# The first extra pass of an expert standing by itself, and a pass's four banks signalled one by one

## The reference

```python
    for e in range(N_EXPERTS):
        h = jax.nn.silu(t @ w1[e]) * (t @ w3[e])
        out = out + gates[:, e:e + 1].astype(t.dtype) * (h @ w2[e])
```

## Time and profile before

| | us |
|---|---|
| runs shown, median of 3 | 1896.12 |
| lowest, highest | 1895.49, 1898.88 |
| the profiled execution, its own time | 1899.83 |
| its span, from first to last instruction | 1897.9 |
| PE busy | 1732.2 (91%) |
| PEld busy | 896.1 (47%) |
| DVE busy | 684.4 (36%) |
| ACT busy | 455.2 (24%) |
| POOL busy | 148.5 (8%) |

### The profile page before, as it was taken

The page is one execution under the profiler, slowest core; times in us unless marked ns, Lnnn a source line. Parts: engine busy times, 40 slices in busy tenths (PEclk is TensorE's granted clock), DMA queues, the critical chain, the costliest instruction groups (busy, mean ns, idle before and its releaser), DMA issues. The chain is left out here.

```text
span 1897.9 us, 24245 instructions
## 1 busy us (share of the span) xinstructions
PE 1732.2 (91%) x9138; PEld 896.1 (47%) x9138; DVE 684.4 (36%) x1403; ACT 455.2 (24%) x894; POOL 148.5 (8%) x113
## 2 busy tenths in 40 slices
PE   8998979998898888889899998999989998899996
PEld 7866643333574443333344544333358767433332
DVE  3344462221415562222312226222144435542223
ACT  2674211111214111111211101111123934111111
POOL 1024100000300100000020100000030131100000
PEclk9999989999999889999999998999999999899998
DMA  9521069999932369679964327899983220589994
GB/s 336 186 108 46 27 268 403 426 425 425 339 144 108 126 269 382 251 313 424 405 236 162 126 115 329 327 424 425 423 304 140 109 90 2 200 351 427 425 426 191
DMA packets 86426, 505.08 MB, mean 266 GB/s; under 512 B 8515, under 2 KB 16756, under 8 KB 59388
## 3 DMA queue, kind: packets, MB, share of 16 engines
q1 hardware_dynamic: 75248, 488.65, 64.0%
q10 hardware_dynamic: 11020, 14.07, 2.2%
HBM read 501.64 MB, written 1.06 MB: 265 GB/s over the span
## 5 line engine op out<-in xcount | busy, mean ns | idle before, releaser
L2028 PE MATMUL bank<-ring,work 128*64 128x512 f32 x1280 | 371.5, 603 | 21.6 <-issue 21.6
L1543 DVE TENSOR_TENSOR work<-bank,work 64x512 f32<-64x512 f32 x64 | 67.9, 1061 | 525.0 <-ACT work L986 524.9
L1693 PE MATMUL bank<-HT,ring 128*128 128x256 f32 x1024 | 232.6, 387 | 0.0
L2028 PEld LDWEIGHTS bank<-ring,work 128*64 128x64 f32 x1280 | 119.5, 139 | 226.0 <-issue 225.5
L1693 PEld LDWEIGHTS bank<-HT,ring 128*128 128x128 f32 x1024 | 199.2, 195 | 37.4 <-issue 10.2
L2072 PE MATMUL bank<-ring,work 128*64 128x512 f32 x896 | 198.9, 595 | 0.0
L1701 PE MATMUL bank<-ring,HT 128*128 128x512 f32 x448 | 198.3, 602 | 0.0
L2028 PE MATMUL bank<-work 128*64 128x512 f32 x320 | 145.1, 603 | 0.0
L986 ACT ACTIVATE work<-bank 64x512 f32<-64x512 f32 x64 | 37.6, 588 | 437.3 <-PE bank L2028 437.3
L2028 PE MATMUL bank<-early_slot,work 128*64 128x512 f32 x320 | 140.7, 592 | 1.1 <-issue 1.1
L1701 PEld LDWEIGHTS bank<-ring,HT 128*128 128x128 f32 x448 | 85.7, 194 | 104.1 <-issue 104.1
(11 more groups left out here) (311 smaller groups left out, 1822.7 us busy)
## 6 DMA issues: line engine op xcount, KB each, us to landing
ring<-in_e_w SPq DMA_DIRECT2D x136, 2048.0 KB, 15.6
early_slot<-in_e_w SPq DMA_DIRECT2D x20, 2048.0 KB, 17.3
work<-in_e_w SPq DMA_DIRECT2D x20, 2048.0 KB, 18.4
ring<-in_a_w_in SPq DMA_DIRECT2D x15, 2048.0 KB, 19.7
work<-in_e_w SPq DMA_DIRECT2D x16, 1024.0 KB, 12.4
HT<-in_e_w SPq DMA_DIRECT2D x16, 1024.0 KB, 15.0
ring<-in_c_w_in SPq DMA_DIRECT2D x8, 2048.0 KB, 21.5
ring<-in_b_w_in SPq DMA_DIRECT2D x6, 2048.0 KB, 25.6
```

The source lines that it names most:

```text
L1543: v.tensor_tensor(by_m(h_[j]), bank[b][CAP:, :], sil[j][CAP:, :], ALU.mult).then_inc(drained[b], 1)
L1693: ins = mm(dst[:, 0:SEQ], wt[:, k, n * P:(n + 1) * P], HT[:, k, :], start=k == 0, stop=k == KC - 1)
L2028: ins = mm(bank[b][lo:lo + CAP, :], x[:, k, :], wt[k], start=k == 0, stop=k == KC - 1, skip_group_check=True)
```

## The change

The pass's code becomes a function, `one_pass(n)`, on each of the three engines. It is called once with n = 1 straight inside `if counted[j] > CAP`; behind that stands `if counted[j] > CAP + Q`, and in it the loop, from n = 2, with the old comparison and a second copy of the pass. A new semaphore, `pass_added`, counts the adds of banks: PE signals `baton` with each of its four last products (so a pass has 12 steps), DVE waits for one, adds that bank, signals `pass_added`, and so on to bank 7. PE and DVE keep a register `added` beside `steps_done`. `scatter` waits at bank b for the add of bank b only; `compact` and the end of `pair` on DVE wait for all. Four small memsets at the start on DVE give `pass_added` its first four counts.

```diff
-PASS_STEPS = 10
+PASS_STEPS = 12
...
+        pass_added = sem("pass_added")
...
# ACT
                         with act.If(counted[j] > CAP):
-                            with act.Fori(1, PASSES) as n:
-                                with act.If(counted[j] > n * Q + Q):
-                                    b0 = act.snap(steps_done)
...
+                            def one_pass(n):
+                                b0 = act.snap(steps_done)
...
+                            one_pass(1)
+                            with act.If(counted[j] > CAP + Q):
+                                with act.Fori(2, PASSES) as n:
+                                    with act.If(counted[j] > n * Q + Q):
+                                        one_pass(n)
# DVE, over_sel
-                        b0 = dve.snap(steps_done)
+                        b0, a0 = dve.snap(steps_done), dve.snap(added)
                         dve.wait_ge(baton, b0)
+                        dve.wait_ge(pass_added, a0)
# DVE, the pass
                         with dve.If(counted[j] > CAP):
-                            with dve.Fori(1, PASSES) as n:
-                                with dve.If(counted[j] > n * Q + Q):
-                                    with dve.If(n > 1):
-                                        over_sel(it, j, n)
...
-                                    dve.wait_ge(h_ready, 2 * nres)
-                                    dve.wait_ge(baton, b0 + (more + 9))
-                                    for b in range(4, 8):
-                                        ins = v.tensor_tensor(part(b), bank[b][:, :], part(b), ALU.add)
-                                    ins.then_inc(baton, 1)
-                                    dve.reg_add(steps_done, steps_done, PASS_STEPS + more)
+                            def one_pass(n):
+                                b0 = dve.snap(steps_done)
...
+                                dve.wait_ge(h_ready, 2 * nres)
+                                for b in range(4, 8):
+                                    dve.wait_ge(baton, b0 + (more + 5 + b))
+                                    v.tensor_tensor(part(b), bank[b][:, :], part(b), ALU.add).then_inc(pass_added, 1)
+                                dve.reg_add(steps_done, steps_done, PASS_STEPS + more)
+                                dve.reg_add(added, added, 4)
+
+                            one_pass(1)
+                            with dve.If(counted[j] > CAP + Q):
+                                with dve.Fori(2, PASSES) as n:
+                                    with dve.If(counted[j] > n * Q + Q):
+                                        over_sel(it, j, n)
+                                        one_pass(n)
...
-                    steps = dve.snap(steps_done)
-                    dve.wait_ge(baton, steps)
+                    a0 = dve.snap(added)
+                    dve.wait_ge(pass_added, a0)
# DVE, at the start
+            for tt in range(TT):
+                for n in range(2):
+                    v.memset(place[:, tt, E + n:E + n + 1], -1.0).then_inc(pass_added, 1)
+            dve.wait_ge(pass_added, 4)
# PE, scatter and compact
-                    steps = pe.snap(steps_done)
-                    pe.wait_ge(baton, steps)
+                    a0 = pe.snap(added)
                     pe.wait_ge(sel_ready, s + (ready + 3))
...
                             pe.wait_ge(drained[b], s + first[b])
+                            pe.wait_ge(pass_added, a0 + (b - 4))
...
-                    steps = pe.snap(steps_done)
-                    pe.wait_ge(baton, steps)
+                    a0 = pe.snap(added)
+                    pe.wait_ge(pass_added, a0 + 3)
# PE, the pass
                         with pe.If(counted[j] > CAP):
-                            with pe.Fori(1, PASSES) as n:
-                                with pe.If(counted[j] > n * Q + Q):
...
-                                            ins = mm(bank[4 + 2 * tt + nh][:, :], m_turned[rr, tt * P:(tt + 1) * P], m_y[rr, :], start=True, stop=True)
-                                    ins.then_inc(baton, 1)
-                                    pe.reg_add(steps_done, steps_done, PASS_STEPS + more)
+                            def one_pass(n):
...
+                                        mm(bank[4 + 2 * tt + nh][:, :], m_turned[rr, tt * P:(tt + 1) * P], m_y[rr, :], start=True, stop=True).then_inc(baton, 1)
+                                pe.reg_add(steps_done, steps_done, PASS_STEPS + more)
+                                pe.reg_add(added, added, 4)
+
+                            one_pass(1)
+                            with pe.If(counted[j] > CAP + Q):
+                                with pe.Fori(2, PASSES) as n:
+                                    with pe.If(counted[j] > n * Q + Q):
+                                        one_pass(n)
```

More of the change, by code:

```diff
@@ new lines, in one_pass @@
+                            def one_pass(n):
+                                b0 = dve.snap(steps_done)
+                                if lead:
+                                    dve.wait_ge(baton, b0 + 2)
+                                    v.tensor_tensor(m_x, bank[4][:, 0:SEQ].rearrange("p (k c) -> p k c", k=KC), columns(g_col, Q), ALU.mult).then_inc(baton, 1)
+                                    dve.wait_ge(baton, b0 + 3)
+                                    v.tensor_tensor(m_x, m_x, columns(b_col, Q), ALU.add).then_inc(baton, 1)
+                                dve.wait_ge(baton, b0 + (more + 3))
+                                v.tensor_tensor(by_m(m_h[:, 0:SEQ]), bank[5][CAP:, 0:SEQ], m_sil[CAP:, 0:SEQ], ALU.mult).then_inc(baton, 1)
+                                dve.wait_ge(h_ready, 2 * nres)
[4 more added lines that the diff above has]
+                                dve.reg_add(added, added, 4)
@@ L1602, in _ @@
             own.then(v.memset(starts[:, :], 0))
+            added = dve.alloc_register("added_dve")
+            dve.reg_mov(added, 4)
             v.memset(place[:, :, :], -1.0).then_inc(baton, 1)
             dve.wait_ge(baton, 1)
+            for tt in range(TT):
+                for n in range(2):
+                    v.memset(place[:, tt, E + n:E + n + 1], -1.0).then_inc(pass_added, 1)
+            dve.wait_ge(pass_added, 4)
             ht_chunks(0)
@@ L2152, in pair @@
                         with pe.If(counted[j] > CAP):
-                            with pe.Fori(1, PASSES) as n:
-                                with pe.If(counted[j] > n * Q + Q):
-                                    b0 = pe.snap(steps_done)
-                                    for b in range(4, 8):
-                                        pass_free(b)
-                                    pe.wait_ge(baton, b0 + 1)
-                                    if lead:
-                                        for k in range(KC):
-                                            for tt in range(TT):
-                                                ins = mm(bank[4][:, k * Q:(k + 1) * Q], XH[:, tt, k * P:(k + 1) * P], m_sel[:, tt, :], start=tt == 0, stop=tt == TT - 1)
-                                        ins.then_inc(baton, 1)
-                                        pe.wait_ge(baton, b0 + 4)
-                                    narrow_up(5, m_x, w1, w3).then_inc(baton, 1)
-                                    pe.wait_ge(baton, b0 + (more + 4))
-                                    narrow_turn(6).then_inc(baton, 1)
-                                    pe.wait_ge(baton, b0 + (more + 6))
-                                    w2 = weights(4 + j)
-                                    narrow_down(7, w2).then_inc(baton, 1)
-                                    pe.wait_ge(baton, b0 + (more + 8))
-                                    for tt in range(TT):
-                                        for nh in range(2):
-                                            rr = slice(nh * CAP, (nh + 1) * CAP)
-                                            ins = mm(bank[4 + 2 * tt + nh][:, :], m_turned[rr, tt * P:(tt + 1) * P], m_y[rr, :], start=True, stop=True)
-                                    ins.then_inc(baton, 1)
-                                    pe.reg_add(steps_done, steps_done, PASS_STEPS + more)
@@ new lines, in one_pass @@
+                            def one_pass(n):
+                                b0 = pe.snap(steps_done)
+                                for b in range(4, 8):
+                                    pass_free(b)
+                                pe.wait_ge(baton, b0 + 1)
+                                if lead:
+                                    for k in range(KC):
+                                        for tt in range(TT):
+                                            ins = mm(bank[4][:, k * Q:(k + 1) * Q], XH[:, tt, k * P:(k + 1) * P], m_sel[:, tt, :], start=tt == 0, stop=tt == TT - 1)
+                                    ins.then_inc(baton, 1)
+                                    pe.wait_ge(baton, b0 + 4)
```

(15 more changed lines are left out.)

22 lines of the change are left out of this document (7 added, 15 removed).

## The result

The changed kernel takes **1986.65 us** (median of 4, 1984.89 to 1994.27), the kernel before 1895.80 beside it; the ratio is 1.0483, 95% interval 1.0458 to 1.0508. The forecast was 1991.0, in a range of 1925 to 2070. The profiled execution took 1994.27 us, with a span of 1992.4 and a mean granted clock of 0.947; before it was 1897.9 and 0.961.

The account below looks back on a forecast made before the run. PE's matmuls were taken as the bound, the weight stream close behind. From the profiled 1899.8 us, -9.4 + 85 + 41 - 17.7 - 3.5 gave 1995, or 1991 us against the median; range 1925 to 2070.

Parts of the forecast that it names:

- The loop, -9.4 us: PE's idle behind the four extra passes, put down to five empty loop rounds each; all 9.4 us expected to go.
- The signals, register waits, second bodies of ACT and DVE at nothing: Extra waits on PE and second pass copies on ACT and DVE, costed at nothing, as hidden under queued matmuls or waiting.
- Jumps beyond two fetched blocks, +85 us: PE's jumps over the doubled pass: 49 would leave the fetched blocks, each losing 1.9 us in the mean; 85 us.
- The second jump of a pair, +41 us: PE's second jump comes while a fetch is under way; waiting for it would add 83 us, otherwise 0; middle taken, 41.
- Late weights swallowed, -17.7 us: PE's waits before up products in the last pairs of layers 0, 2 and 3, 17.7 us, vanish as PE runs later.
- Idle of kind (3), -3.5 us: PE's two idle times before the turn at L2036, 1.93 and 1.55 us, taken off as already in the jump count.
- The clock, nothing in the sum: Lower granted clock after PE idles of over 2.4 us: 1.5 us lost each for 25, counted only in rival (c).
- rival (c): Every second jump pays 3.3 us and long idles bring the clock down: about 2070 us, chance 0.12.
- Rival (a): PE's fetcher goes further ahead than two blocks, so longer jumps cost nothing more: 1889 us, faster, chance 0.10.
- Rival (b): Jumps miss but fetches take only 3.4 us, as weight traffic thins: about 1900 to 1915 us, chance 0.10.

Follow-up runs that it names:

- one_body_one_signal: Kernel before, with PE's loop made to end at the expert's count and one signal for all four banks kept: 1892.64 us, ratio 0.9989.
- first_only: Kernel after, with the second part (loop over passes 2 and on) left out on PE, ACT and DVE: 1882.02 us, ratio 0.9911.
- pe_one_body: Kernel after, but PE has one pass body in a loop ending at the expert's count; ACT and DVE keep two: 1888.26 us, again 1884.12.
- dead_half: Kernel before, with only one up-projection of a pass (140 instructions) as never-run copy on PE: 1951.39 us, ratio 1.0303.
- dead_copy: Kernel before, with a second, never-run copy of the pass body behind the loop on PE alone: 2018.71 us, ratio 1.0638.
- two_hops: Kernel after, with the second part on PE behind the first if instead of inside it, so two jumps over one body each: 2042.01 us, ratio 1.0725.

## Why the prediction was right, and where by luck

The sign, the mechanism and the total were right: 1986.65 against 1991.0. By its own steps:

- **The loop, -9.4 us**: -9.9 by start-to-start time. Right, and for the reason given: with the loop's rounds gone alone DVE's adds are late next, 2.22 and 2.3 us, and the signals take that away. That warning was only argued there; one_body_one_signal shows it.
- **The signals, register waits, second bodies of ACT and DVE at nothing**: right, as far as the measurement can tell. first_only has the signals and pe_one_body all of them, and both are faster than before.
- **Jumps beyond two fetched blocks, +85 us**: 97.5. 49 were counted; 44 take over 5.5 us, and PE shows new idle at 43 places. The price was too low: 1.9 us was taken from two jumps, both ahead of a turn, and 43 places of 97.5 us make 2.27 each. New idles ahead of a turn cost 2.2 us in the mean, those ahead of an up product 2.4, where 0.2 us more pass between the branch's end and the matmul. The mechanism has been tried from four sides: a copy that never runs (47 jumps, 2018.7 us), half of one (27, as computed from its length, or 33 by the packets), two short hops, and the early hint. dead_half bears most: it set apart blocks left from length crossed.
- **The second jump of a pair, +41 us**, the middle between 0 and 83: this step failed. It is near 0. Where one fetch was still on its way at a second jump, it delayed next to nothing: at 377.1 us another fetch packet starts 0.03 us behind the jump, and the jump's own starts at 4.03 and its branch ends after 6.37, as for a first jump (307.2: 3.87 and 6.28). Both are under way together. Of the 25 long second jumps 11 met a packet that started between 1.4 us before them and 0.6 behind; they took 6.37 us in the mean, the other 14 took 6.17, and in dead_copy both kinds took 6.15, where 3.3 more were forecast. That the following fetch comes about 6 us behind the first was right for half of the cases: its packet starts 3.1 to 4.3 us behind the first's own in 10 of 19 first jumps, 5.0 to 6.0 in the others. A middle between two ends that a single row in the trace could not decide was a number for a thing that didn't happen. What it stood for exists elsewhere: in two_hops the first hop needs the pending block before it can go on, and there the waits do add.
- **Late weights swallowed, -17.7 us**: right in size, and in the cause: each of the nine waits of before ends within 0.3 us of the landing of a weight piece. At four of the nine places PE doesn't wait any more, at the other five it now stands for the jump instead, 10.6 us, which is in the 97.5.
- **Idle of kind (3), -3.5 us**: it was not two places but five. The reading left out the three at 732.8, 1172.0 and 1298.2 us, 7.9 us in all, which wait for code without a jump. By start-to-start time the two lose 1.5 us and the three 6.0, and one new wait of the same sort adds 2.4.
- **The clock, nothing in the sum**, only in rival (c), with 25 x 1.5 us: it costs 30.8 us net; the 17 stretches behind the new idles lose 1.5 to 1.8 us each, two of them 3.0 and 3.1. This was seen in the earlier trace rows and given to a rival; it belonged into every case in which PE stands still 40 times more.

So 41 us that were not there were made up by 12.5 more at the jumps and 30.8 of the clock; the errors of +41 and -43 nearly cancelled, and the distance of 4 us says little of how good the sum was. The range, 1925 to 2070, was about what this sum could carry.

Rival (a), a fetcher further ahead, is ruled out: the branch at 307.2 took 6.28 us. The Trainium skill (Runtime: NRT & Kernel Launch, Instruction fetch mechanics) has both the window of two blocks, with which the traces agree to within seven jumps (44, 47 and 27 take over 5.5 us in the kernel after, dead_copy and dead_half, and 55, 57 and 33 have a packet that starts 0.8 us or more behind the branch, where the window gives 49, 50 and 27), and the larger PE store, with which none of these runs agrees. Rival (b), cheap misses, did not come: with the DMA share still at 0.80 to 0.91 the jumps take 5.7 to 6.9 us. Jumps of 3.3 to 4.4 us, as the one at 267.4 in the earlier trace rows, come mostly at the start and the end of a stage; their packet starts some 1 us behind the branch and not 3.4 to 4.5.

Open: of the 6.2 us of a jump beside the weight stream some 4 pass before the fetch packet starts and 1.4 behind its end. What fills the first 4, the queue beside the weights' or the request, no run took apart. Taking the pass out of the main line of PE's code, so that the common path jumps over nothing, wasn't tried.

## What to carry to other kernels

Code that never runs has a price on the engine that jumps over it: count the instructions between a branch and its target, and compare that with what the engine holds. A second body cost nothing that shows on ScalarE and VectorE, which wait for TensorE most of the time, and 5% on TensorE, which is the bound; a loop that ends at the runtime count needs no second body. And when one wait is removed, run the half-change: here the loop's end and the single signal hid each other, and either one removed alone gained nothing that could be told.

## What was not expected of the hardware

- A branch whose target is not fetched mostly takes 5.7 to 6.9 us beside the weight stream, 3.3 to 4.4 at the start or end of a stage; the fetch packet itself runs for about 1.0 us of it, and the branch ends 1.3 to 1.5 us behind the packet. PE's queue hides about 4.4 us.
- PE can also run on into a block that is not there yet, without a jump: 3.6, 2.0 and 2.3 us in the kernel before, 10.7 us more in dead_copy.
- Two fetches can be under way at once, but two jumps in a row can't: 2.75 + 5.55 us, and 5.85 + 5.66 us, in two_hops.
- A prefetch hint some 5.5 us ahead brought first experts' jumps from 6.1 us to between 0.4 and 4.0 us, and one 2.5 to 3.4 us ahead mostly to about 3; for 23 second experts, whose hint mostly came within 0.9 us of another jump's landing, it did nothing.
- Some 17 of the 43 idles of about 2 us were followed by 2.5 to 6 us at the 1.2 GHz level, 1.5 to 3.1 us lost each time; the slower matmuls begin within 2 us of PE being busy again.
